# Forgetting attention taken into the program of its own projections

## The reference

```python
proj = h @ w_in                      # 1024 x (4*1024 + 8)
q, k, v, z, f_logit = jnp.split(proj, [1024, 2048, 3072, 4096], axis=-1)
c = jnp.cumsum(jax.nn.log_sigmoid(f_logit + b_f), axis=1)      # decay, per head
s = jnp.einsum('bqhd,bkhd->bhqk', q_i, k) / sqrt(128)
logits = jnp.where(k_pos <= q_pos, s + c_q - c_k, -inf)
o = jnp.einsum('bhqk,bkhd->bqhd', softmax(logits), v)
y = (o * jax.nn.silu(z)) @ w_out
x = x + y
```

## Time and profile before

| | |
|---|---|
| median of 3 runs | 2246.73 us |
| profiled execution: time, span | 2247.12, 2245.4 us |
| TensorE busy, share of the span | 2167.7 us, 97% |
| VectorE, ScalarE, GpSimd busy | 51%, 39%, 18% |
| granted clock, mean | 0.981 |
| weight split, ScalarE (L286), VectorE (L296), mean of one | 1.04, 1.27 us |
| landing of a 512 KB tile: fox_in, gdn_in (median) | 11.5, 4.1 us |
| attention: reciprocal (L1234), scaling of 256 keys (L1236), read of the row maximum | 0.159, 0.353, 0.083 us |
| 32 mask selects on GpSimd (L2324) | 18.4 us |

### The profile page before, as it was taken

How to read it: one execution, slowest core, us unless ns; L and a number is a source line. 1 busy time by engine, 2 the same in 40 slices (tenths; PEclk the granted TensorE clock), 3 DMA queues, 4 the chain that set the end, 5 groups by cost and what they waited for, 6 DMA issues and landing times. The chain is left out here.

```text
span 2245.4 us, 29101 instructions
## 1 busy us (share of the span) xinstructions
PE 2167.7 (97%) x10810; PEld 1750.9 (78%) x10810; DVE 1141.6 (51%) x1823; ACT 866.2 (39%) x1422; POOL 413.1 (18%) x454
## 2 busy tenths in 40 slices
PE   7999999999999999999899999999999998999999
PEld 6888887766677888888788878886788887886667
DVE  5444323644466444323575544335566686665444
ACT  4322223564334222223432233225446753543453
POOL 2111101212324111000220010001110242024441
PEclk9999999999999999999999999999999997999999
DMA  4333333611112333333233346750143211243111
GB/s 143 112 94 95 101 94 83 112 47 57 57 47 76 110 95 93 106 94 88 66 106 95 94 72 104 93 97 11 48 127 90 67 50 36 67 109 66 48 47 47
DMA packets 359450, 182.13 MB, mean 81 GB/s; under 512 B 42053, under 2 KB 356142, under 8 KB 358958
## 3 DMA queue, kind: packets, MB, share of 16 engines
q1 hardware_dynamic: 359000, 180.57, 32.2%
q10 hardware_dynamic: 342, 0.12, 0.0%
HBM read 176.14 MB, written 4.52 MB: 80 GB/s over the span
## 5 line engine op out<-in xcount | busy, mean ns | idle before, releaser
L329 PE MATMUL ps<-xh,wh 128*128 128x512 f32 x1904 | 757.7, 398 | 1.5 <-DVE wl L296 1.5
L331 PE MATMUL ps<-xh,wl 128*128 128x512 f32 x1904 | 742.4, 390 | 0.0
L330 PE MATMUL ps<-xl,wh 128*128 128x512 f32 x1904 | 741.5, 389 | 0.0
L296 DVE TENSOR_TENSOR wl<-raw,wh 128x1024 fp32r<-128x1024 f32 x328 | 416.4, 1270 | 400.7 <-ACT wh L286 395.6
L286 ACT ACTIVATE wh<-raw 128x1024 fp32r<-128x1024 f32 x328 | 341.3, 1043 | 359.9 <-PE ps L331 313.2
L329 PEld LDWEIGHTS ps<-xh,wh 128*128 128x128 f32 x1904 | 357.5, 188 | 83.7 <-issue 10.6
L331 PEld LDWEIGHTS ps<-xh,wl 128*128 128x128 f32 x1904 | 357.4, 188 | 76.3
L330 PEld LDWEIGHTS ps<-xl,wh 128*128 128x128 f32 x1904 | 357.8, 188 | 72.4 <-issue 2.4
L471 POOL TENSOR_TENSOR acc<-acc,sq 128x512 f32<-128x512 f32 x72 | 101.6, 1412 | 258.8 <-ACT sq L913 166.2
L478 PE MATMUL ps<-xh,wh 128*128 128x512 f32 x288 | 121.1, 421 | 20.9 <-ACT xh L410 8.1
L329 PE MATMUL ps<-a_hi,wh 128*128 128x512 f32 x352 | 137.0, 389 | 0.0
(11 more groups left out here) (414 smaller groups left out, 2547.7 us busy)
## 6 DMA issues: line engine op xcount, KB each, us to landing
raw<-in_w_ffn_gate SPq DMA_DIRECT2D x44, 512.0 KB, 3.8
raw<-in_w_ffn_up SPq DMA_DIRECT2D x44, 512.0 KB, 3.8
raw<-in_w_ffn_down SPq DMA_DIRECT2D x32, 512.0 KB, 3.9
raw<-in_conv_w_in SPq DMA_DIRECT2D x32, 512.0 KB, 4.0
raw<-in_fox_w_in SPq DMA_DIRECT2D x32, 512.0 KB, 11.5
raw<-in_gdn_w_in SPq DMA_DIRECT2D x32, 512.0 KB, 4.1
raw<-in_w_in SPq DMA_DIRECT2D x24, 512.0 KB, 3.8
raw<-in_swa_w_in SPq DMA_DIRECT2D x32, 256.0 KB, 3.8
```

The lines of the kernel that those rows point to most:

```text
L296: nc.vector.tensor_tensor(wl[s][:, 0:kb, :], raw[r][:, 0:kb, :], wh[s][:, 0:kb, :].bitcast(F32), ALU.subtract).then_inc(lo_done, 1)
L329: pe.matmul(o, wh[s][:, kb, :], x_hi, start=start, stop=False)
L330: pe.matmul(o, wh[s][:, kb, :], x_lo, start=False, stop=False)
L331: return pe.matmul(o, wl[s][:, kb, :], x_hi, start=False, stop=stop)
```

## The change

- The forget tile is tile 0; tiles 1 to 24 are q, k, v of head 0, of head 1 and so on; the 8 gate tiles are 25 to 32. `fox_in` is written out, without a loop.
- q and k are kept for two heads (`fox_qk`), v before and after its transposition for two; q's scale is taken in at the evacuation.
- The decay's chain lies beside tiles 0 to 2. Each head's value transposes and decay rows share bank 7.
- The units run in order of the heads, inside the projection: with k = 4 + 3 x head, transposes and decay rows in tile k, units 0 and 1 of the head in tile k+1, unit 2 in k+2, unit 3 in k+3. Scores use banks 2 and 3, transposes 4 and 5, the value products bank 6 alone, one group for each head.
- Gates (silu, product, split into own buffers `fox_o_hi`, `fox_o_lo`) lie beside tiles 29 to 32, the last two after them. `fox_out` goes on in the same block, without a barrier.
- Buffers: the 32 x 512 columns of `fox_qkvz` are replaced by smaller ones.

```diff
@@ steps
-            if full < 4 or name in ("swa_in", "mix_in", "gdn_in", "ple") or name.endswith("_down"):
+            if full < 4 or name in ("swa_in", "mix_in", "gdn_in", "fox_in", "ple") or name.endswith("_down"):
@@ the forgetting layer
+            groups = [(TB * hd + TB - 1, F[:, hd, :], lambda b: b[:, :]) for hd in range(H8)]
+            at_pe, at_dve, at_act = softmax_steps("fox", units, groups, room, c, ((2, 3), (4, 5), (6,)))
+            plan = {}
+            for hd in range(H8):
+                k = 4 + 3 * hd
+                for at, what in ((k, [("t", hd), ("d", hd)]), (k + 1, [("c", 4 * hd), ("c", 4 * hd + 1)]),
+                                 (k + 2, [("c", 4 * hd + 2)]), (k + 3, [("c", 4 * hd + 3)])):
+                    plan[at] = plan.get(at, []) + what
+            for x in range(4):
+                plan[29 + x] = [("c", U + x)]
...
+                for u in range(U):
+                    hd, qb = u // TB, u % TB
+                    w = (qb + 1) * P
+                    pool.wait_ge(decay_in, hd + 1)
+                    if u >= 2:
+                        pool.wait_ge(z_done, u_fox + u - 1)
+                    nc.gpsimd.affine_select(out=slot[:, u % 2, 0:w], in_=decay[:, hd % 2, 0:w], ...)
...
+            def pe_do(pe, kind, x):
+                if kind == "t":
+                    pe.wait_ge(evac, ev0 + 3 * x + 4)
+                    if x:
+                        pe.wait_ge(decay_in, x)
+                    for t in range(TB):
+                        m = pe.transpose(ps[VT][:, t * P:t * P + P], vf[:, x % 2, t * P:t * P + P], ident[:, :])
+                    m.then_inc(turned, 1)
+                elif kind == "d":
+                    if x == 0:
+                        pe.wait_ge(fsel, 4)
+                        pe.wait_ge(fd, 9)
+                    pe.wait_ge(taken, turned0 + x + 1)
+                    pe.matmul(ps[VT][:, :], nsel[:, x, :], fhl[:, :], start=True, stop=True).then_inc(decay_mm, 1)
+                else:
+                    ...
+                    at_pe(pe, x)
...
+            def pe_amid(pe, k, b):
+                todo = plan.get(k, [])
+                for q, (kind, x) in enumerate(todo):
+                    if (q + 1) * DB // len(todo) - 1 == b:
+                        pe_do(pe, kind, x)
...
+            def dve_amid(dve, k):
+                if k == 2:
+                    dve.wait_ge(fsel, 4)
+                    dve.wait_ge(fd, 4)
...   (minimum, scan, cast, difference, cast, as before)
+                for kind, x in plan.get(k, []):
+                    dve_do(dve, kind, x)
+                for b in {30: (0, 1), 31: (2, 3), 32: (4, 5)}.get(k, ()):
+                    gate(dve, b)
+                for b in {31: (0, 1), 32: (2, 3)}.get(k, ()):
+                    low(dve, b)
+            def act_amid(act, k):
+                if k == 1:
+                    act.preload_act_table_set("natural_log_exp_and_others")
...   (absolute value, exponential, logarithm, as before)
+                for kind, x in plan.get(k, []):
+                    act_do(act, kind, x)
+                for b in {29: (0, 1, 2, 3), 30: (4,), 31: (5,), 32: (6,)}.get(k, ()):
+                    silu(act, b)
+                for b in {30: (0, 1), 31: (2, 3), 32: (4, 5)}.get(k, ()):
+                    high(act, b)
...
+            def x_act(act):
+                silu(act, 7)
+                for b in (6, 7):
+                    high(act, b)
+            def x_dve(dve):
+                gate(dve, 6)
+                low(dve, 4)
+                low(dve, 5)
+                gate(dve, 7)
+                low(dve, 6)
+                low(dve, 7)
-            sums, block, pro = resid_out("fox_out", *gate_x(lambda b: qkv[:, 24 + b, :]), gain=..., joint=joint)
+            sums, block, pro = resid_out("fox_out", x_act, x_dve, gain=..., block=block, x_hi=oh, x_lo=ol)
```

More of the change, by code:

```diff
@@ L109, in src @@
             def src(i, j):
[L110 to L115, removed]
+                k = 4 * i + j
+                if k == 0:
+                    return [(0, H8, v, 4 * D)]
+                return [(0, P, v, fox_block(k) * P)]
             return src
@@ L2191, in kernel_program, with head_v @@
             fhl = sb("fox_f_parts", [LO + H8, SEQ], F32R, ctx=c)
-            decay = sb("fox_decay", [P, 4, SEQ], ctx=c)
+            decay = sb("fox_decay", [P, 2, SEQ], ctx=c)
             f_in, fsel, fd, decay_mm, decay_in, bias_in = (sem(f"fox_{x}") for x in ("bf", "sel", "f", "rows", "decay", "bias"))
-            ev0 = n["ev"]
-            turn = token_turn(lambda b: qkv[:, 16 + b, :], 8, vt, lambda b: (evac, ev0 + 16 + b + 1))
+            ev0, turned0, x0, fs0 = n["ev"], n["lots"], n["x"], n["fs"]
+            n["lots"] += H8
+            n["x"] += DB
+            n["fs"] += DB
+            VT = 7
+            def head_v(hd):
+                return slice(hd % 2 * P, hd % 2 * P + P)
+            units = []
+            for u in range(TB * H8):
+                hd, qb = u // TB, u % TB
+                klen = (qb + 1) * P
+                units.append(dict(
+                    q=qk[:, hd % 2, 0, qb * P:qb * P + P], k=qk[:, hd % 2, 1, 0:klen], klen=klen,
+                    mask=slot[:, u % 2, 0:klen], mask_ready=(bias_in, u + 1), po=0, m=P,
+                    oc=qb * P, v=[vt[:, x, head_v(hd)] for x in range(qb + 1)]))
+            groups = [(TB * hd + TB - 1, F[:, hd, :], lambda b: b[:, :]) for hd in range(H8)]
+            u_fox = n["units"]
+            at_pe, at_dve, at_act = softmax_steps("fox", units, groups, room, c, ((2, 3), (4, 5), (6,)))
+            U = len(units)
+            plan = {}
[6 more added lines that the diff above has]
+                plan[29 + x] = [("c", U + x)]
             def sp_tail(sp):
@@ L2220, in pe_beside @@
[L2220 to L2226, removed]
-            def dve_beside(dve, k):
[L2229 to L2236, removed]
+                for u in range(U):
+                    hd, qb = u // TB, u % TB
+                    w = (qb + 1) * P
+                    pool.wait_ge(decay_in, hd + 1)
+                    if u >= 2:
+                        pool.wait_ge(z_done, u_fox + u - 1)
+                    nc.gpsimd.affine_select(out=slot[:, u % 2, 0:w], in_=decay[:, hd % 2, 0:w], compare_op=ALU.is_ge,
+                                            fill=-NEG, base=qb * P, pattern=[[-1, w]], channel_multiplier=1).then_inc(bias_in, 1)
@@ new lines, in bank @@
+            def bank(k):
+                return HEAD if k == 4 * DB else two_banks(k)
+            def f_evac(dve, i, j, ev0_):
+                k = 4 * i + j
+                src = ps[bank(k)]
+                hd, part = (k - 1) // 3, (k - 1) % 3
+                if k == 0:
+                    nc.vector.tensor_tensor(fl[:, 0, :], src[0:H8, :], rstd[0:H8, :], ALU.mult).then_inc(evac, 1)
+                elif k > 3 * H8:
+                    nc.vector.tensor_tensor(zs[:, k - 3 * H8 - 1, :], src[:, :], rstd[:, :], ALU.mult).then_inc(evac, 1)
+                elif part == 0:
+                    if hd >= 2:
+                        dve.wait_ge(scored, u_fox + TB * (hd - 1))
+                    nc.vector.scalar_tensor_tensor(out=qk[:, hd % 2, 0, :], in0=src[:, :], scalar=-(P ** -0.5), in1=rstd[:, :],
+                                                   op0=ALU.mult, op1=ALU.mult).then_inc(evac, 1)
+                elif part == 1:
+                    nc.vector.tensor_tensor(qk[:, hd % 2, 1, :], src[:, :], rstd[:, :], ALU.mult).then_inc(evac, 1)
+                else:
+                    if hd >= 2:
+                        dve.wait_ge(turned, turned0 + hd - 1)
+                    nc.vector.tensor_tensor(vf[:, hd % 2, :], src[:, :], rstd[:, :], ALU.mult).then_inc(evac, 1)
@@ new lines, in pe_do @@
+            def pe_do(pe, kind, x):
[13 more added lines that the diff above has]
+                else:
+                    if x < U and x % TB == 0:
+                        pe.wait_ge(evac, ev0 + 3 * (x // TB) + 4)
+                    if 3 <= x < U + 3 and (x - 3) % TB == 0:
+                        pe.wait_ge(taken, turned0 + (x - 3) // TB + 1)
+                    at_pe(pe, x)
@@ new lines, in dve_do, with act_do @@
+            def dve_do(dve, kind, x):
+                if kind == "t":
+                    if x >= 2:
+                        dve.wait_ge(pv_done, u_fox + TB * (x - 1))
+                    dve.wait_ge(turned, turned0 + x + 1)
+                    nc.vector.tensor_copy(vt[:, :, head_v(x)], ps[VT].rearrange("p (t q) -> p t q", t=TB)).then_inc(taken, 1)
+                elif kind == "c":
+                    at_dve(dve, x)
+            def act_do(act, kind, x):
+                if kind == "d":
+                    if x >= 2:
+                        act.wait_ge(bias_in, TB * (x - 1))
+                    act.wait_ge(decay_mm, x + 1)
+                    nc.scalar.activation(decay[:, x % 2, :], ps[VT][:, :], ACT.Copy).then_inc(decay_in, 1)
+                elif kind == "c":
+                    at_act(act, x)
```

(8 more changed lines are left out.)

61 lines of the change are left out of this document (27 added, 34 removed).

## The result

The changed kernel took 2250.91 us in the median (2249.45 to 2255.78, 20 runs), the kernel before 2247.38 us on the same chips (2245.64 to 2252.8, 20 runs): a ratio of 1.0015, 95% interval 1.0008 to 1.0021. The gain of 19.2 us in the stretch was used up, as forecast (2249.8), and a little more. The profiled execution took 2253.34 us with a span of 2251.6, 2.4 over its kernel's median.

A forecast was written before the change was run, and what follows sets the result against it. TensorE, at 97% of the span, was taken as the bound. Terms -19.2 + 11.2 (a) + 4.1 + 1.7 (b) + 5.3 (c) gave +3.1 us on 2246.73: 2249.8 us, 8-in-10 range 2240.5 to 2256.5.

The forecast's parts named there:

- the stretch: From the end of the projection's first three tiles to the start of the fourth output tile: 248.7 us before the change.
- What goes: -19.2: Forgetting-attention stretch: all TensorE overhead (two pauses, low clock, decay parts, waits between short units) goes, 19.2 us.
- (a): 35 spots where units interrupt projection matmuls, plus eight decay matmuls: changes of operand kind add 11.2 us.
- the floor: TensorE's necessary work in the stretch (projection, attention blocks, transposes, decay matmuls, output head): 229.5 us, unchanged by the change.
- (b): Attention's start: head 0's value transposes wait 4.1 us for tile 3's evacuation behind VectorE's chain; low clock adds 1.7.
- (c): Single value-product bank: TensorE waits 0.9 us for VectorE's copy out in each of heads 1 to 6, 5.3 us.
- (d): Everything else at nothing: queries' scaling, weights landing in 11.5 us at the median against three tiles of lead, forget tile.
- No wait of (b) or (c): First rival, at the start and value bank: neither wait appears, -8.0, 2238.7 us; chance 0.12.
- Masks delaying the weight split: Second rival, in each head: GpSimd's mask delays VectorE's split ahead of the copy out, +6.4, 2256.2 us; chance 0.11.
- Dearer spots: Third rival, transposes inside the units: 0.15 us more in each of 35 spots, +5.3, 2255.1 us; chance 0.10.

The follow-up runs named there:

- experiment 2: Changed kernel with tiles 1 to 3 reading neighbouring column blocks (queries of heads 0 to 2) instead of q, k, v of head 0: 2246.73 us, ratio 1.0.
- experiment 1: Kernel before with only its projection tiles ordered by head and written out without a loop, forget tile still 28th: 2252.77 us, ratio 1.0026.
- experiment 6: experiment 4 with the forget tile third instead of first (q, k of head 0, forget tile, v of head 0): 2244.61 us, ratio 0.9987.
- experiment 4: Changed kernel with the decay's chain on VectorE moved behind tile 3's evacuation, head 0's decay rows and first units later: 2245.76 us, ratio 0.9994.

## Why the prediction was right in the time, and where its steps were wrong

The time was 1.1 us off and the verdict as forecast, but by luck: inside the stretch the forecast was 3.1 too high, and 5.8 came in front of it that no term had.

**What goes: -19.2.** Right. Between tile 32 and the first output matmul lie 0.23 us, at a clock of 1.00, and the waits between short units are gone. With the measured terms below (wait, clock, bank, operands, pace) the stretch is 229.5 + 4.2 + 3.0 + 7.4 + 2.6 + 1.5 = 248.2; the trace has 248.69, so 0.5 is not placed.

**(a) Changes of operand kind, +11.2: mis-sized; the measured term is +4.1.** This unit is one without a wait, in the timeline of after:

```profile
1444.12 0.39 PE L335 MATMUL ps<-xh,wl 128*128 128x512 f32 x1
1444.35 0.38 PE L1199 MATMUL ps<-fox_qk 128*128 128x128 f32 x2
1444.57 0.49 PE L1206 MATMUL ps<-ident,fox_room 128*128 128x128 f32 x3
1444.90 0.61 PE L1217 MATMUL ps<-fox_room,fox_v 128*128 128x128 f32 x4
1445.27 0.47 PE L333 MATMUL ps<-xh,wh 128*128 128x512 f32 x1
1445.58 0.39 PE L334 MATMUL ps<-xl,wh 128*128 128x512 f32 x1
```

The matmul ahead of the score takes 0.23 (no entry price). The four value records take 0.37 where 4 x 0.111 would be 0.44 (-0.08), and the projection matmul behind them 0.31 (+0.08): the two cancel, and a spot costs about 0.01, 35 of them 0.3. I had carried the price over from a stage whose scores have 64 rows, and had taken it to come with every change between fp32 and rounded fp32. Only the decays, with 40, pay it: 0.29 each on top of the 0.33 that is in the floor, 2.3 in all (forecast 1.6). One small cost I did not look for: counted over the trace, the second to tenth projection matmul behind a unit or a decay take 0.2306 in the mean instead of 0.2267. Over the 387 of them in the stretch at full clock that is 1.5 us. The kernel before has it as well: behind the unit of the earlier trace rows, after the 0.34, the starts are 0.24, 0.22 and 0.24 apart. Its cause stays open.

**(b) The start: wait 4.1 right to the tenth, clock mis-sized.** VectorE's timeline is the queue that I had added up: its chain, the evacuation of tile 2, a split, the evacuation of tile 3.

```profile
1384.13 0.67 DVE L2353 SCALAR_TENSOR_TENSOR fox_f<-fox_f 8x512 f32<-8x512 f32 x1
...
1387.69 0.69 DVE L2276 TENSOR_TENSOR fox_qk<-ps,rstd 128x512 f32<-128x512 f32 x1
...
1389.43 0.68 DVE L2280 TENSOR_TENSOR fox_vf<-ps,rstd 128x512 f32<-128x512 f32 x1
```

The chain took 3.56 (3.55 forecast). The clock was at 0.50 for 6.8 us, of which TensorE worked 6.0 (1390.17 to 1396.2; the rest was the end of the pause), not 3.4, so it cost 3.0 instead of 1.7. From start to start the wait is 4.2 (4.44 less one matmul). In experiment 2 the same pause had only 3.4 us (1384.0 to 1387.4) at 0.50 behind it, so the pause alone doesn't fix the size; what does is not shown.

**(c) The value bank: six waits, heads 1 to 6, as forecast; mis-sized.** The profile counts 1.1 each and the timeline 1.23: 7.4 instead of 5.3. VectorE's copy ended where I had put it, 5.2 after the third unit's start (forecast 5.3; 1430.74 to 1435.93), but TensorE was there after 4.1 and not 4.5, since its unit paid less than (a) had charged. So most of this error follows from that of (a).

**(d) "The rest at nothing", with the weights landing in 11.5 us: this step failed.** It measured +5.8. The median of the page's list is that of the whole layer; at its start, where the next layer's first tiles are fetched behind the convolution's, hold no landing at all, and I did not read those four DMAs: 14.4 us, used the moment they landed. The median of the layer in fact fell to 8.1 (8.9 in experiment 1), while tile 2, the one on the path, rose from 14.5 to 17.9. That the order of tiles is also an order of addresses was not in the sum.

**The rivals.** No wait of (b) or (c): both waits were there. Masks delaying the weight split: no split beside the heads took more than 1.23 us, and none of the stretch's 33 splits overlapped a select in time, as my count had it. What the Trainium skill (SBUF — State Buffer, Who interferes with whom) says of VectorE and GpSimd shutting each other out was thus not put to the test here. Dearer spots: transposes inside a unit take 0.11 each (0.33 for three, 1444.57 to 1444.90).

In the stretch, +3.1 forecast and 0.0 measured, the forecast was 7.1 too much for (a), 1.4 too little for (b) and 2.1 for (c), with 0.5 not placed. In front of it (d) missed 5.8; the unchanged parts differ by +1.3 and -0.9, together the 6.2 of the spans. In the medians the change is +3.5.

## What to carry to other kernels

When a change reorders tiles, look at the first few transfers of the stage by themselves, with the time at which each is needed; a median over the stage says nothing of them. Here the first tiles landed sooner from neighbouring columns, while the median over the layer was lower with the distant ones. Take a price for switching only from operands of the same shape. In an engine's program order, an instruction that frees a bank goes ahead of a split that waits for another engine: that one line was worth 5 us.

## What the runs showed of the hardware, unexpected

- Of the stage's first three or four 512 KB tiles the median to landing was 14.4 to 14.5 us from neighbouring columns and 17.4 to 18.4 from columns 1024 apart, in every kernel run. Neighbours are not always fast: in the kernel before, tiles asked for at 1372 to 1382 took 15.2 to 18.5, where the changed kernel's took 8.7 to 10.6.
- A 32 KB tile landed in 4.6 us ahead of the full ones and in 16.1 behind them.
- One matmul with operands of 40 rows between matmuls of 128 rows cost 0.39 us more than one of 128 rows. A whole unit of fp32 matmuls between rounded fp32 ones, all of 128 rows, cost about 0.01 in its changes.
- Pauses of 3.5 to 5.5 us were followed by 3.4 us at half clock in some places (experiment 6 at the head, experiment 2 at the start of the attention) and by about 6 in others (the changed kernel, at the head and at the start of the attention); the 0.5 left in experiment 4, and the 1.1 in experiment 2, by none.
